# Value projection of a hybrid diffusion layer: token tiles stationary, the 256 value columns moving

## The reference, cut to what matters

```python
h = rms_norm(x, lp['norm1_g']) * (1 + sc1) + sh1
proj = h @ lp['w_in']
q, k, v, xp, ga, gb = jnp.split(proj, cuts, axis=-1)
...
v = v.reshape(b, l, N_KV_HEADS, HEAD_DIM)          # 2 heads of 128: 256 value columns
k_ctx_out, v_ctx_out = k, v                        # context rows are also outputs (new cache)
v_all = jnp.concatenate([ctx_kv[1], v], axis=1)    # 512 cached rows join for the latent tokens
attn = block_attention(q, k_all, v_all)
```

## Time and profile before

| | us |
|---|---|
| median of 3 runs (1817.8 to 1820.91) | 1819.08 |
| the profiled execution's own time | 1816.4 |
| its span, first to last instruction | 1814.5 |
| TensorE matmul busy | 1616.6 (89%) |
| TensorE weight load busy | 1278.2 (70%) |
| VectorE busy | 898.6 (50%) |
| ScalarE busy | 593.2 (33%) |
| GpSimd busy | 393.8 (22%) |
| mean granted TensorE clock | 0.953 of full |

### The profile page before, as it was taken

How to read it: one execution, slowest core, us unless ns; L and a number is a source line. 1 busy time by engine, 2 the same in 40 slices (tenths; PEclk the granted TensorE clock), 3 DMA queues, 4 the chain that set the end, 5 groups by cost and what they waited for, 6 DMA issues and landing times. The chain is left out here.

```text
span 1814.5 us, 22464 instructions
## 1 busy us (share of the span) xinstructions
PE 1616.6 (89%) x8410; PEld 1278.2 (70%) x8410; DVE 898.6 (50%) x1257; ACT 593.2 (33%) x764; POOL 393.8 (22%) x252
## 2 busy tenths in 40 slices
PE   4899999999999699999999899989977399999950
PEld 4688888878887466666666588878866288888840
DVE  5560000006565666676666543341147667666638
ACT  5211121232222444444444500021123055555513
POOL 1011111112223400000000121121116234445420
PEclk8999999999999899999999999999998599999985
DMA  8133434230100500000000133213032179898945
GB/s 350 67 115 135 159 132 143 109 119 23 46 23 9 200 1 0 0 1 1 0 0 0 58 139 121 85 53 124 23 114 105 65 233 295 266 290 277 281 77 218
DMA packets 38016, 202.28 MB, mean 111 GB/s; under 512 B 4304, under 2 KB 5072, under 8 KB 27728
## 3 DMA queue, kind: packets, MB, share of 16 engines
q1 hardware_dynamic: 28752, 168.07, 24.0%
q0 software_dynamic: 9216, 33.56, 8.3%
HBM read 154.43 MB, written 47.19 MB: 111 GB/s over the span
## 5 line engine op out<-in xcount | busy, mean ns | idle before, releaser
L324 PE MATMUL psum<-h_hi,w_hi 128*128 128x512 f32 (+1 forms) x768 | 199.3, 368 | 7.3 <-DVE h_lo L624 5.5
L324 PE MATMUL psum<-h_lo,w_hi 128*128 128x512 f32 (+1 forms) x768 | 193.6, 361 | 0.0
L324 PE MATMUL psum<-h_hi,w_lo 128*128 128x512 f32 (+1 forms) x768 | 192.5, 359 | 0.0
L885 PE MATMUL psum<-probT,vals 128*128 128x512 f32 x384 | 190.9, 593 | 0.0
L946 ACT ACTIVATE prob<-psum,nmax 128x1536 f32<-128x1536 f32 x64 | 98.6, 1541 | 209.5 <-DVE nmax L1025 209.5
L324 PEld LDWEIGHTS psum<-h_hi,w_hi 128*128 128x128 f32 x768 | 128.7, 190 | 34.7 <-issue 14.3
L539 POOL TENSOR_TENSOR w_lo<-w_raw,w_hi 128x1024 fp32r<-128x1024 f32 x32 | 77.0, 2408 | 348.2 <-ACT w_hi L451 348.2
L901 PEld LDWEIGHTS psum<-ident,prob 128*128 128x128 f32 x768 | 93.0, 141 | 78.6 <-issue 72.7
L324 PEld LDWEIGHTS psum<-h_lo,w_hi 128*128 128x128 f32 x768 | 128.8, 190 | 23.1
L324 PEld LDWEIGHTS psum<-h_hi,w_lo 128*128 128x128 f32 x768 | 128.5, 189 | 23.1
L1022 DVE TENSOR_REDUCE rmax<-psum 128x1 f32<-128x512 f32 x192 | 128.9, 688 | 31.1 <-PE psum L877 30.8
(11 more groups left out here) (326 smaller groups left out, 3026.3 us busy)
## 6 DMA issues: line engine op xcount, KB each, us to landing
gu_raw<-in_w_gu SPq DMA_DIRECT2D x16, 2048.0 KB, 9.4
ada<-in_w_ada SPq DMA_DIRECT2D x20, 1024.0 KB, 4.8
w_raw<-in_w_in SPq DMA_DIRECT2D x16, 1024.0 KB, 4.8
dn_raw<-in_w_dn SPq DMA_DIRECT2D x16, 1024.0 KB, 6.9
gates<-gst SPq DMA_DIRECT2D x16, 640.0 KB, 3.0
wm_raw<-in_w_merge SPq DMA_DIRECT2D x4, 1536.0 KB, 7.8
y_sum<-stage SPq DMA_DIRECT2D x12, 512.0 KB, 11.9
xt<-in_x SPq DMA_DIRECT2D x10, 512.0 KB, 8.0
```

The costliest lines, as they stand in the source:

```text
L324: mm = pe.matmul(psum[:, par_sets[j] + g:par_sets[j] + g + w], a[j][:, k, :], b[:, k, g:g + w], start=(k == 0 and a is w_hi and b is h_hi) ...
L885: mm = pe.matmul(psum[:, PV + 512 * x.par:PV + 512 * x.par + 512], vals[:, x.key0 // P + c, x.kv * HD:(x.kv + 1) * HD], probT[b][g % 2][:] ...
```

## The change

The value projection is turned around. The matmul's stationary operand is now a tile of 128 tokens of `h`, and the moving operand is the 256 value columns of both halves, read as two runs of 128. The result comes out with tokens on the partitions, 256 columns for each of ten tiles, packed in PSUM columns 0 to 2559. There are 24 matmuls a tile (8 chunks, 3 products). Two tiles at a time are copied straight to `vals`; the `vraw` copies and the transposes are gone. The two halves of each weight part are made neighbours in one tensor, `v_hi` and `v_lo`. TensorE now waits for both halves' weights before its first value matmul; the hooks of key half 1 come after token tiles 1 and 3; the free second PSUM set is asked for before tile 6. SyncE's order at the end becomes: `cache_v` after `k_lo`, one store of `out_v` straight from `vals` after ScalarE's first copy, `cache_k` after the last value matmul. GpSimd's list is unchanged.

```diff
-        w_hi = [at(f"w_hi{j}", [P, KC, P], F32R, RW + (8 + 8 * j) * KB) for j in range(2)]
-        w_lo = [at(f"w_lo{j}", [P, KC, P], F32R, RW + (12 + 8 * j) * KB) for j in range(2)]
+        v_hi = at("v_hi", [P, 2, KC, P], F32R, RW + 8 * KB)
+        v_lo = at("v_lo", [P, 2, KC, P], F32R, RW + 16 * KB)
+        w_hi, w_lo = ([v[:, j] for j in range(2)] for v in (v_hi, v_lo))
...
+        def v_pair(p):
+
+            return vals[:, 2 * p:2 * p + 2, :].rearrange("p t n -> p (t n)"), psum[:, 512 * p:512 * (p + 1)]
...
-                for j in range(2):
-                    sp.wait_ge(s["v_raw"], j + 1)
-                    if j == 1:
-                        sp.dma_start(kc_raw[:], io["cache_k"]).then_inc(s["cache_in"], 16)
-                        sp.wait_ge(s["k_fin"], 2)
-                        sp.dma_start(vals[:, TILES:KEY_TILES, :], io["cache_v"]).then_inc(s["cache_in"], 16)
-                    sp.dma_start(io["out_v"][j], vraw[j][:, 0:CTX]).then_inc(s["vout"], 16)
                 sp.wait_ge(s["kout"], 32)
-                sp.wait_ge(s["vout"], 32)
+                sp.wait_ge(s["k_lo"], 2)
+                sp.dma_start(vals[:, TILES:KEY_TILES, :], io["cache_v"]).then_inc(s["cache_in"], 16)
+                sp.wait_ge(s["v_out_a"], 1)
+                sp.dma_start(io["out_v"].rearrange("(t p) n -> p t n", p=P), vals[:, 0:CTX_TILES, :]).then_inc(s["vout"], 16)
+                sp.wait_ge(s["v_mm"], TILES)
+                sp.dma_start(kc_raw[:], io["cache_k"]).then_inc(s["cache_in"], 16)
+                sp.wait_ge(s["vout"], 16)
...
                 project(K0, 1, hooks=hooks(4, 0))
-                project(V0, 0, hooks=hooks(4, 1))
-                project(V0, 1)
-
+
+                def v_tile(t):
+
+                    o = psum[:, t * KV * HD:(t + 1) * KV * HD]
+                    h = slice(t * P, (t + 1) * P)
+                    for k in range(KC):
+                        pe.matmul(o, h_hi[:, k, h], v_hi[:, :, k, :], start=(k == 0), stop=False)
+                        pe.matmul(o, h_hi[:, k, h], v_lo[:, :, k, :], start=False, stop=False)
+                        mm = pe.matmul(o, h_lo[:, k, h], v_hi[:, :, k, :], start=False, stop=(k == KC - 1))
+                    mm.then_inc(s["v_mm"], 1)
                 for j in range(2):
-                    pe.wait_ge(s["v_raw"], j + 1)
...
+                    pe.wait_ge(s[f"w_hi{j}"], V0 + 1)
+                    pe.wait_ge(s[f"w_lo{j}"], V0 + 1)
+                pe.wait_ge(s["ps_free0"], V0)
+                for t in range(TILES):
+                    if t == 6:
+                        pe.wait_ge(s["ps_free1"], V0)
+                    v_tile(t)
+                    if t == 1:
+                        sums(4, 1)
+                    if t == 3:
+                        spread(4, 1)
...
-                act.wait_ge(s["k_lo"], 2)
-                act.wait_ge(s["kout"], 32)
-                for j in range(2):
-                    act.wait_ge(s[f"mm{j}"], V0 + 1)
...
-                    nc.scalar.copy(vraw[j][:], psum[:, par_sets[j]:par_sets[j] + TOK]).then_inc(s["v_raw"], 1)
                 act.wait_ge(s["q_fin"], HEADS)
                 act.wait_ge(s["k_fin"], 2)
...
+                for p in range(0, HALF, 2):
+                    act.wait_ge(s["v_mm"], 2 * p + 2)
+                    nc.scalar.copy(*v_pair(p)).then_inc(s["v_out_a"], 1)
...
+                dve.wait_ge(s["k_lo"], 2)
+                for p in range(1, HALF, 2):
+                    dve.wait_ge(s["v_mm"], 2 * p + 2)
+                    nc.vector.tensor_copy(*v_pair(p)).then_inc(s["v_out_d"], 1)
```

More of the change, by code:

```diff
@@ L149, in build @@
         kraw = [stage, at("kraw1", [P, TOK], F32, RKV + 40 * KB)]
-        vraw = [stage, at("vraw1", [P, TOK], F32, RHL)]
         kc_raw = at("kc_raw", [P, KV, PAST], F32, RHL + 8 * KB)
@@ L156, in build @@
                   "d_done gate_r0 gate_r1 gate_st0 gate_st1 py_ps py_out py_st sq_r0 sq_r1 ss_mm rt_sq rt_r rs_mm rs_out q_raw q_sin q_cos q_fin "
-                  "k_fin k_hi k_lo kout v_raw vout v_ps v_out_a v_out_d cache_in cache_hi cache_lo dve_c").split():
+                  "k_fin k_hi k_lo kout vout v_mm v_out_a v_out_d cache_in cache_hi cache_lo dve_c").split():
             s[n] = sem("b1_" + n)
@@ L404, in _ @@
                 project(K0, 1, hooks=hooks(4, 0))
-                project(V0, 0, hooks=hooks(4, 1))
-                project(V0, 1)
-                for j in range(2):
-                    pe.wait_ge(s["v_raw"], j + 1)
[L410 to L419, removed]
+                def v_tile(t):
[6 more added lines that the diff above has]
+                    mm.then_inc(s["v_mm"], 1)
+                for j in range(2):
+                    pe.wait_ge(s[f"w_hi{j}"], V0 + 1)
[9 more added lines that the diff above has]
+                        spread(4, 1)
             @block.scalar
@@ L518, in _ @@
                     nc.scalar.copy(kT_hi[:, j, 0:TOK], kraw[j][:]).then_inc(s["k_hi"], 1)
-                act.wait_ge(s["k_lo"], 2)
-                act.wait_ge(s["kout"], 32)
-                for j in range(2):
-                    act.wait_ge(s[f"mm{j}"], V0 + 1)
-                    if j == 1:
-                        act.wait_ge(s["mm1"], V0 + 1)
-                    nc.scalar.copy(vraw[j][:], psum[:, par_sets[j]:par_sets[j] + TOK]).then_inc(s["v_raw"], 1)
                 act.wait_ge(s["q_fin"], HEADS)
                 act.wait_ge(s["k_fin"], 2)
-                for n in range(0, 6, 2):
-                    act.wait_ge(s["v_ps"], n + 1)
-                    nc.scalar.copy(*v_chunk(n)).then_inc(s["v_out_a"], 1)
+                for p in range(0, HALF, 2):
+                    act.wait_ge(s["v_mm"], 2 * p + 2)
+                    nc.scalar.copy(*v_pair(p)).then_inc(s["v_out_a"], 1)
                 act.wait_ge(s["cache_in"], 32)
@@ L741, in _ @@
                     dve.sem_inc(s["k_fin"], 1)
-                for n in range(1, 6, 2):
-                    dve.wait_ge(s["v_ps"], n + 1)
-                    nc.vector.tensor_copy(*v_chunk(n)).then_inc(s["v_out_d"], 1)
+                dve.wait_ge(s["k_lo"], 2)
+                for p in range(1, HALF, 2):
+                    dve.wait_ge(s["v_mm"], 2 * p + 2)
+                    nc.vector.tensor_copy(*v_pair(p)).then_inc(s["v_out_d"], 1)
         if last_block == 1:
@@ L2082 @@
     io = {name: nc.dram_tensor("in_" + name, a.shape, f32, kind="ExternalInput").ap() for name, a in arrays.items()}
-    for name, shape in (("y", (TOK, D)), ("out_k", (KV, HD, CTX)), ("out_v", (KV, HD, CTX))):
+    for name, shape in (("y", (TOK, D)), ("out_k", (KV, HD, CTX)), ("out_v", (CTX, KV * HD))):
         io[name] = nc.dram_tensor(name, shape, f32, kind="ExternalOutput").ap()
@@ L2088 @@
     r = _run(nc, [{"in_" + name: a for name, a in arrays.items()}], core_ids=[0]).results[0]
-    cache = [r[name].transpose(2, 0, 1).reshape(1, 1, CTX, KV, HD) for name in ("out_k", "out_v")]
+    cache = [r["out_k"].transpose(2, 0, 1).reshape(1, 1, CTX, KV, HD), r["out_v"].reshape(1, 1, CTX, KV, HD)]
     return r["y"][:CTX].reshape(1, CTX, D), r["y"][CTX:].reshape(1, LAT, D), cache[0], cache[1]
```

## The result

The changed kernel takes 1829.38 us (median of 5 runs, 1828.6 to 1829.83), the kernel before 1820.91 us in 5 runs (1817.8 to 1821.5; three of them are the runs whose median was the time before). The ratio is 1.0051, 95% interval 1.0036 to 1.0065: slower by 8.5 us by the medians and by 9.2 by the means. The forecast was 1829.

A forecast was written before the change was run, and what follows sets the result against it. TensorE is busy 89%, but key half 1's chain sets the first block's end: 12.1 later, minus 1.9 in the tail, is 10.2; 1816.4 becomes 1826.6, plus 2.7 to the median gives 1829.3, said 1829, range 1825 to 1834 us.

The forecast's parts named there:

- late start of the values: TensorE's first value matmul waits for half 1's low weights until 563.3 instead of starting at 553.50: 9.8 us late.
- half clock: After the new gap TensorE runs 2.9 us at clock 0.50, losing 1.45 us; bounds none and 2.75.
- hooks: Key half 1's sums and spread each come after two value tiles, 5.71 us instead of 5.27: together 0.88 us later.
- `spread` later, in all: Key half 1's spread on TensorE starts 9.8 + 1.45 + 0.88 = 12.1 us later, at 578.4.
- saved in the tail: From the last kT_lo to the last cache load's issue takes 0.9 us instead of 2.81: 1.9 us saved.
- block's end: First block ends 12.1 - 1.9 = 10.2 us later.
- The matmul term: 240 value matmuls at 0.119 us make 28.6 us against 28.1 before: the same work to half a microsecond.
- the rival of slower matmuls: Value matmuls each cost their weight load, 0.190 us, 45.6 us in all; block ends 23.6 us late, 1843; chance 0.05.
- The rule on weight loads: Loads overlap matmuls only for another row group, so 96 more value-projection loads would cost about 10 us more; prediction sided against it.
- The cover: TensorE's last value matmul ends 2.2 us ahead of key half 1's last kT_lo; thin but there.
- The landing of `cache_k`: The block's last load lands 4.8 us after issue, with 128 KB more ahead of it; bounds 3.9 and about 5.2.
- all of it stays: Behind the barrier after the first block nothing changes or waits for a slower party, so the whole 10.2 us stays.

The follow-up runs named there:

- run 2: Changed kernel plus 70 unused matmuls in the gap before the first value matmul, holding the clock; 1826.88 us, ratio 1.0030.
- run 1: Changed kernel with GpSimd making the low weights of value half 1 before the cosine product of key half 0; 1825.48 us, ratio 1.0026.
- run 3: Changed kernel with key half 1's sums moved into the gap before the first value tile and spread behind tile 0; 1822.32 us, ratio 1.0007.
- run 4: Changed kernel with the out_v store issued behind the load of cache_k instead of ahead of it; 1828.65 us, ratio 1.0044.
- second and third profiles of before: The kernel before, unchanged, profiled two more times, one execution each; 1821.11 and 1818.69 us.
- run 5: Changed kernel with GpSimd's low weights of half 1 first and the sums in the gap, spread behind tile 2; 1817.36 us, ratio 0.9983.
- run 6: run 5 with cached keys loaded early over the raw weights and split earlier, cached values loaded after the key rotation; 1811.03 us, ratio 0.9954.
- run 7: Kernel before, keeping its value projection, copies and transposes, with run 6's tail and GpSimd order, half 0's copy moved ahead; 1808.49 us, ratio 0.9942.
- run 8: run 6 plus 25 unused matmuls around the sums, spread behind tile 1, value copies not waiting for k_lo; 1807.64 us, ratio 0.9932.

## Why the prediction was right, point by point

Each term beside what the profile of the changed kernel shows:

| term | forecast, us | measured, us |
|---|---|---|
| late start of the values | 9.8 | 10.49 - 0.59 = 9.90 |
| half clock | 1.45 | 15.45 - 13.81 = 1.64 (run 2) |
| hooks | 0.88 | 13.81 - 12.77 = 1.04 (run 2 against before) |
| `spread` later, in all | 12.1 | 25.94 - 13.36 = 12.58 |
| `spread` to last `kT_lo` | 20.36 | 598.65 - 578.31 = 20.34 |
| last matmul's end ahead of `kT_lo` | 2.2 | 598.65 - 596.83 = 1.82 |
| saved in the tail | 1.9 | 7.59 - 6.19 = 1.40 |
| block's end | +10.2 | +11.15 |

The 12.77 is from the first value matmul to `spread` before, 566.27 - 553.50. The tail went from 594.22 - 586.63 = 7.59 us between `kT_lo` and the cached keys' cast to 604.84 - 598.65 = 6.19.

**The wait** is shown to be the cause, not only seen: run 1 shortens it and changes nothing else in PE's list, and the stretch follows one for one. **The matmul term** is shown: value matmuls are 0.12 us apart at full clock, 240 times and with the operand in two runs, so the rival of slower matmuls is out. The rule on weight loads that the prediction took from "TensorE: Matmul & The Clock Gate" of the Trainium skill, Part 3, does not hold here: at 0.12 us for load and 256 columns the 96 further loads did not cost the 10 us that it gave. **The hooks** cost nearly what they should: in run 2 the values start at 561.74 and the sums at 567.56, 5.8 us for two tiles. **The cover** of TensorE's end held in the changed kernel and was the bound once the chain was moved (run 3).

**What was off.** The landing of `cache_k` took 5.2 us, the upper bound of that term, where I had taken 4.8; run 4 shows that the store ahead of it in the queue is a good part of that. With its issue 0.08 later than thought, the tail saved 0.50 less. Ahead of the tail `spread` came 0.45 late: 0.10 by the start, 0.19 by the clock, which took 3.8 us from 562.86 to come back and not 2.9, and 0.16 by the hooks. Together the block ends 0.95 later than forecast. The 2.9 us was no fixed price: behind the same gap (8.76 and 8.80 us) the second and third profiles of before stay at half clock for 5.9 us, from 601.82 and 601.79 to about 607.7. Behind the values' gap of 9.7 us the half clock lasted 3.3 to 3.8 us in the three profiles that have it (the changed kernel's two and run 4), so the term's size came out near 1.45; the row that it was read from did not make that certain.

**Where the two errors met.** The forecast of 1829.3 was reached from a base of 1819.08, which was the median of three runs; the base beside the result and the experiments is 1820.0 to 1820.9. The prediction let all of the block's 10.2 us stay in the time; against 1820.91 the change costs 8.5 us, not 10.2, and not the 11.15 of the stretch. So the step "all of it stays" was 1.7 us too high and the base 1.8 too low, and the two cancel. The difference lies outside the stretch, where the code is the same: the profiled execution of before, at 1816.4, was the one with the short attention block. Against the second profile of before, the changed kernel's next block starts 609.66 - 598.82 = 10.8 us later and its span ends 1828.0 - 1819.2 = 8.8 later; 0.8 of the 2.0 between went in the attention. For the rest I can show no cause, and the second and third profiles of before differ by more, with spans of 1819.2 and 1816.8.

So the mechanism and the sum for the block were right, to a microsecond, and that the time itself was met within 0.4 us is chance.

## What to carry to other kernels

Before an operand is widened over two halves that are made one after the other, ask who makes the second half and what stands before it in that engine's list: here the turned matmul was as fast as the old one, copies and transposes were saved, and more was lost to the wait for half 1. Look next at what is queued behind the waiting instruction, since here it was not the values but the key chain that ended the block. And when copies and transposes are taken out of a tail, find first whether they ended it: in the old shape, the two loads, GpSimd's order, the cached keys' cast and one copy put elsewhere shortened the stretch by 8.2 us (the time fell by 11.6), and with the same tail the two shapes can't be told apart by the time.

## What was not expected of the hardware

**Vector and GpSimd products of two tiles slow each other.** One 128 x 1024 subtraction on GpSimd takes 2.34 to 2.40 us with VectorE idle, or when it starts just ahead of VectorE's addition; where VectorE's sine products were under way it takes 3.36 to 3.44 (runs 1, 5, 6, 7, 8), and the four sine products take 7.00 to 7.05 in place of 4.97, or 9.19 to 9.22 with two subtractions beside them. VectorE's 128 x 1024 addition takes 3.40 us in the earlier trace rows, while GpSimd subtracts, and 1.23 in run 1, where GpSimd is idle: before, it ended 1.1 us after the subtraction had. "GPSIMD Engine Reference" of the Trainium skill, section 1, Specifications, says that GpSimd shares its SBUF interfaces with VectorE and contends with VectorE instructions that have two SBUF inputs; the trace agrees, with the numbers above. A subtraction moved into GpSimd's idle time was therefore not free, and it is 1.0 of the 1.2 us by which run 1 fell short.

**The clock's second fall.** In the same kernel, the attention block's first 18 us have the clock at 0.50 once or twice, as the execution has it: the block took 429.9 us with one such time and 433.1 and 433.2 with two. That the second fall makes the whole difference is not shown. One profile of a kernel is thus no base for a difference of 3 us in a block that the change does not touch.
